# An expert layer with sixteen more tokens taken row by row, plain fp32 gate products, and a shared low-half duty

## The chip, the cores and the metric

One core of one Trainium2 chip runs one program. The metric is the time of one execution in microseconds (us). The engines are named PE (TensorE), DVE (VectorE), ACT (ScalarE), POOL (GpSimd) and SP (SyncE, which only issues DMAs here).

## The reference

Two transformer blocks on 512 tokens of width 1024. The part that the change touches is the expert layer of the first block: for each token and each of 8 heads, 16 of 16,384 one-neuron experts are chosen, and

```
act = gelu(einsum('thkd,td->thk', expert_u[experts], xb))
wgt = (g * act)
out = einsum('thk,thkd->td', wgt, expert_v[experts])
```

with `g` the softmax gates. All of it is fp32, and everything downstream depends on it. A token has 128 chosen experts (8 heads by 16).

## The kernel before

Weights come in 456 tiles of 128 x 1024 fp32 (512 KB). SP loads each into one of four slots (`wraw`), ACT rounds it to fp32r (`whi`), and DVE or POOL forms the remainder (`wlo = wraw - whi`). PE then computes each product as three fp32r matmuls: high by high, high by low, low by high (`three`, L1394 to L1396). A slot is loaded again when its low half is counted in the semaphore `w_lo` (SP waits for it in `load_w`), and ACT rewrites a slot of `whi` when PE has finished the tile that used it. PE starts a tile when `w_lo` has counted it.

The expert layer has two ways to do a token.

Densely, for the first SD tokens: 128 tiles of U (`u_blocks`) give the activation of every one of the 16,384 experts for each token, ACT applies gelu and stores the result (`act_dram`, or keeps it in SBUF for the last 20 tiles). The gates are spread over the 16,384 places by a product of two one-hot matrices per token: DVE makes `OI` (index i equals row) and `OG` (index j equals column, times the gate), and PE multiplies them for four tokens at a step (`gate_group`, L1756), which gives a 128 x 128 gate matrix per token. These steps (STEPS = SD/4) run interleaved with 60 of the U tiles, the gate tiles; 5 or 6 eighths of a U tile stand on PE between two steps. ACT and DVE move the products to `GS`, SP stores them (`gate_dram`). Then 128 tiles of V follow: DVE multiplies activations by gates (`pw_product`, L2532), ACT and DVE split the product into high and low (`WH`, `WL`), and PE accumulates over all 128 tiles into its eight banks.

By rows, for the others. The last 128 tokens (one per partition) and the FT "few" tokens before them are not in SD. For these, POOL fetches exactly the rows of U that were chosen, 128 rows of 4 KB at a time (`fetch_u`, L786), DVE makes a dot product with the token (`dot`, L2342), and in the V stage POOL fetches rows of V (`fetch_v`, L793) and DVE adds them with their weight (`row_add`, L2568). A fetch serves 128 pairs of token and expert: the last block takes 128 fetches, and FT few tokens, spread over P/FT partitions each, take FT fetches. Both rings have four buffers, so a fetch waits for the dot or the addition four before it.

So SD = 384 - FT, and with FT = 16 the dense products have 368 columns, there are 92 gate steps, and 144 dots and 144 row additions.

The order of work is written out by hand, one program for each engine. Around the gate steps it is as follows. Before them DVE runs the top-k selection (`topk`) and normalizes the gates (L2439, semaphore `tk_gate`); PE waits for that after U tile 38 (counted from 0) and then transposes gates and indices (L1742 to L1744), does tile 39 and begins with the gate tiles. A DVE step is `indices_hot` (waits for the product of two steps earlier), two `gate_sum` (adding the low half of an earlier product), `gates_hot` (waits for POOL's `OJ`), and a dot every second step. A POOL step is `offsets_j` (L800, at most four ahead), a low half when one is due (60 in the 92 steps), and a fetch every second step. After the gate steps DVE takes over the low halves from tile 103 on and the remaining dots, SP issues the last stores of the gates.

## Time and profile before

| what | value |
|---|---|
| median of three runs | 2395.32 us (2394.99 to 2395.55) |
| the profiled execution's own time | 2394.86 us |
| its span in the profile | 2393.0 us |
| PE busy | 2359.3 us (99%) |
| DVE, POOL, ACT busy | 1559.5, 1249.3, 944.9 us |
| U tiles on PE | from 508.4 to 1076.7 us |
| of these the gate tiles, with the 92 gate steps | 670.3 to 964.8 us |
| V tiles on PE | 1076.7 to 1592 us |

The profile gives for each engine the time in which it executed something. Matmul records overlap: the duration of one includes the way through the array, so what a matmul costs is read from the distance between the starts of two that follow each other.

### The profile page before, as it was taken

The numbers are of one execution on the slowest core, as the hardware profiler recorded it, in microseconds if no ns is written. First come the engines' busy times: TensorE is split into PE (matmuls) and PEld (weight loads), VectorE is DVE, ScalarE is ACT, GpSimd is POOL, SyncE is SP. The second block draws the span as 40 slices with busy tenths as digits, with TensorE's granted clock in tenths as the row PEclk, the third lists the DMA queues.
The fourth block names the chain that finished last, engine by engine and source line by source line (L and its number), as shares of the span: only waits on it lengthen the run. The fifth ranks groups of instructions, "written<-read, shape, count | busy, mean of one in ns | idle before, by whom it ended". The sixth has DMA issues, their size and how long they took to land.

```text
span 2393.0 us, 35812 instructions
## 1 busy us (share of the span) xinstructions
PE 2359.3 (99%) x12844; PEld 2121.5 (89%) x12844; DVE 1559.5 (65%) x2832; ACT 944.9 (39%) x1487; POOL 1249.3 (52%) x705
## 2 busy tenths in 40 slices
PE   7999999999999999999999999999999999999998
PEld 4878888899999999999999999998778888888886
DVE  5258435789999999679999999992365225322201
ACT  4374333344555555333333334442353223222312
POOL 3305443447899999455555555444304444444443
PEclk9999999999999999999999999999999999999999
DMA  7237422338978998999999999943202222222221
GB/s 285 80 115 264 180 93 93 132 117 280 319 240 305 321 326 306 393 379 414 413 416 411 417 406 405 376 162 114 75 23 97 97 97 88 97 96 96 96 98 71
DMA packets 179614, 526.15 MB, mean 220 GB/s; under 512 B 18240, under 2 KB 70896, under 8 KB 178224
## 3 DMA queue, kind: packets, MB, share of 16 engines
q1 hardware_dynamic: 120928, 345.24, 39.7%
q0 software_dynamic: 43024, 159.14, 17.2%
q10 hardware_dynamic: 15552, 20.36, 2.4%
q8 instruction: 63, 1.03, 0.2%
q14 instruction: 47, 0.39, 0.0%
HBM read 474.93 MB, written 49.73 MB: 219 GB/s over the span
## 4 chain that ended last, share of the span: by engine, by line
PE 94%; DVE 2%; DMA 2%; POOL 1%; ACT 1%; issue 0%; SPq 0%; ACTq 0%; DVEq 0%
PE bank L1394 22%; PE bank L1396 22%; PE bank L1395 22%; PE pair L1395 6%; PE pair L1394 6%; PE pair L1396 6%; PE pair L1756 2%; DMA wraw<-in_w 1%; PE bank L1924 1%; PE pair L1535 1%; PE bank L1561 1%; PE bank L1574 1%; POOL wlo L720 1%; PE pair L1697 1%; PE bank L1915 0%; PE bank L1907 0%
## 5 line engine op out<-in xcount | busy, mean ns | idle before, releaser
L720 POOL TENSOR_TENSOR wlo<-wraw,whi 128x1024 fp32r<-128x1024 f32 x303 | 741.4, 2450 | 743.6 <-ACT whi L867 742.3
L1394 PE MATMUL bank<-HH,whi 128*128 128x512 f32 (+1 forms) x2048 | 739.3, 361 | 4.8 <-ACT T L1139 2.1
L1396 PE MATMUL bank<-HH,wlo 128*128 128x512 f32 (+1 forms) x2048 | 735.9, 359 | 0.0
L1395 PE MATMUL bank<-HL,whi 128*128 128x512 f32 (+1 forms) x2048 | 735.8, 359 | 0.0
L867 ACT ACTIVATE whi<-wraw 128x1024 fp32r<-128x1024 f32 x456 | 481.8, 1058 | 617.0 <-PE pair L1396 308.0
L1394 PEld LDWEIGHTS bank<-HH,whi 128*128 128x128 f32 x2048 | 385.1, 188 | 47.5 <-issue 7.2
L1396 PEld LDWEIGHTS bank<-HH,wlo 128*128 128x128 f32 x2048 | 384.7, 188 | 40.2
L1395 PEld LDWEIGHTS bank<-HL,whi 128*128 128x128 f32 x2048 | 385.2, 188 | 39.3 <-issue 0.2
L793 POOL DMA_INDIRECT VROW<-in_w,which x128 | 204.6, 1599 | 191.5 <-DVE YROW L2568 178.7
L2500 DVE TENSOR_TENSOR wlo<-wraw,whi 128x1024 fp32r<-128x1024 f32 x153 | 186.3, 1218 | 20.5 <-ACT whi L867 18.7
L786 POOL DMA_INDIRECT X<-in_u_rows,which x128 | 149.9, 1171 | 60.4 <-DVE dots L2342 34.3
L1394 PE MATMUL bank<-WH,whi 128*128 128x368 f32 x512 | 169.0, 330 | 0.0
L1395 PE MATMUL pair<-WL,whi 128*128 128x368 f32 x512 | 168.8, 330 | 0.0
L1394 PE MATMUL pair<-WH,whi 128*128 128x368 f32 x512 | 168.7, 329 | 0.0
L1396 PE MATMUL bank<-WH,wlo 128*128 128x368 f32 x512 | 168.4, 329 | 0.0
L1395 PE MATMUL bank<-WL,whi 128*128 128x368 f32 x512 | 168.3, 329 | 0.0
L1396 PE MATMUL pair<-WH,wlo 128*128 128x368 f32 x512 | 168.1, 328 | 0.0
L2568 DVE SCALAR_TENSOR_TENSOR YROW<-VROW,wexp,YROW 128x1024 f32<-128x1024 f32 x128 | 165.6, 1294 | 0.4 <-DMA VROW<-in_w,which 0.2
L2616 DVE TENSOR_TENSOR T<-bank,rr 128x512 f32<-128x512 f32 x60 | 41.3, 690 | 179.9 <-PE bank L1396 179.8
L2472 DVE SCALAR_TENSOR_TENSOR OG<-T,pair 128x1024 fp32r<-128x1024 f32 x92 | 111.5, 1212 | 11.7 <-POOL T L800 11.7
L1077 ACT ACTIVATE actb<-bank 128x368 f32<-128x368 f32 x108 | 51.7, 479 | 144.7 <-PE bank L1396 137.2
L1147 ACT ACTIVATE WH<-AJ 128x368 fp32r<-128x368 f32 x128 | 64.9, 507 | 81.2 <-DVE AJ L2532 74.7
(444 smaller groups left out, 3826.2 us busy)
## 6 DMA issues: line engine op xcount, KB each, us to landing
wraw<-in_w SPq DMA_DIRECT2D x456, 512.0 KB
gate_dram<-GS SPq DMA_DIRECT2D x24, 1024.0 KB
GJ<-gate_dram SPq DMA_DIRECT2D x32, 768.0 KB
act_dram<-actb ACTq DMA_DIRECT2D x108, 184.0 KB
AJ<-act_dram SPq DMA_DIRECT2D x108, 184.0 KB
adaw<-in_ada SPq DMA_DIRECT2D x32, 512.0 KB
ada<-in_ada SPq DMA_DIRECT2D x16, 512.0 KB, 14.8
NB<-in_nab POOLq DMA_DIRECT2D x4, 1024.0 KB
```

Source lines behind the costliest of these rows:

```text
L720: nc.gpsimd.tensor_tensor(wlo[:, slot, :, :].rearrange("p k c -> p (k c)"), wraw[:, slot, :, :].rearrange("p k c -> p (k c)"), whi[:, slot ...
L786: pool.indirect_dma_start(UROW[:, m % R, :], None, A["u_rows"], bass.IndirectOffsetOnAxis(row_index(0, dot_column(m)), 0)).then_inc(u_row[ ...
L793: pool.indirect_dma_start(VROW[:, n % R, :], None, A["w"].rearrange("g p c -> (g p) c"), bass.IndirectOffsetOnAxis(row_index(1, V_ROWS[n]) ...
L867: nc.scalar.activation(whi[:, slot, :, :].rearrange("p k c -> p (k c)"), wraw[:, slot, :, :].rearrange("p k c -> p (k c)"), ACT.Copy).then ...
L1077: nc.scalar.activation(actb[:, u % 2, :], bank[u % 2][:, 0:SD], ACT.Gelu_apprx_tanh).then_inc(tile_evac, 1)
L1147: nc.scalar.activation(WH[:, slot, :], AJ[:, slot, 0:SD], ACT.Copy).then_inc(pw_hi, 1)
L1394: pe.matmul(out_, ah, bh, start=first, stop=False, **kw)
L1395: pe.matmul(out_, ah, bl, start=False, stop=False, **kw)
L1396: return pe.matmul(out_, al, bh, start=False, stop=last, **kw)
L2472: nc.vector.scalar_tensor_tensor(OG[:, q % 2, :, :, :].rearrange("p w t j -> p w (t j)"), bc(oj, 1, 2), 0.0, bc(gate_window[:, P + 8 * n:P ...
L2500: nc.vector.tensor_tensor(wlo[:, slot, :, :].rearrange("p k c -> p (k c)"), wraw[:, slot, :, :].rearrange("p k c -> p (k c)"), whi[:, slot ...
L2568: nc.vector.scalar_tensor_tensor(y, VROW[:, n % R, :], w, y, ALU.mult, ALU.add).then_inc(row_added, 1)
```

## The change

Six things change together.

- FT is 32, not 16: SD is 352, there are 88 gate steps, and 160 dots and 160 row additions. A few token now lies on 4 partitions. In the V stage a few row is added after every third row of the last block, up to tile 95, where it was every seventh, up to tile 111.
- The gates are no longer split into high and low. The gate products are plain fp32 matmuls with 128 columns, four at a step, where they were fp32r matmuls with 256 columns (both halves side by side), also four. `OG` has half its width.
- ACT alone moves the products of a step to `GS`, in one copy of 512 elements; before, a step took two copies of 256 elements on ACT and two additions of the same size on DVE.
- 92 dots stand at the gate steps (46 before), 32 in the tail of the U tiles (38 before), and 8 in the V stage (32 before).
- Of the 60 low halves at the gate steps, DVE makes the 30 of odd tiles, at the step of the tile, ahead of that step's one-hot matrices. They are not counted in `w_lo` by DVE: POOL waits for DVE's own count when it comes to the low half of the next tile, and then counts with a small `memset`.
- The last gate group stands three eighths into the U tile that follows the gate tiles, where it stood behind it. The fifth block of gates is stored from load 61 on instead of 59.

```
-FT = 16
+FT = 32
...
+U_TAIL = 4 * GATE_IT + GATE_TILES + 3
+U_POOL = 103
...
-GATE_DOT = 2
-PSUM_DOTS = TOP_DOTS + STEPS // GATE_DOT
-U_DOTS = 112
+GATE_DOTS = 92
+PSUM_DOTS = TOP_DOTS + GATE_DOTS
+TAIL_DOTS = 32
+U_DOTS = PSUM_DOTS + TAIL_DOTS
...
+        def low_step(t):
+            return (t - 4 * GATE_IT - 3) * STEPS // GATE_TILES + 1
...
 # POOL
+            def vector_low(t):
+                passed[0] += 1
+                pool.wait_ge(w_low_vector, passed[0])
+                pool.wait_ge(w_lo, G0["U"] + t)
+                nc.gpsimd.memset(low_mark, 0.0).then_inc(w_lo, 1)
...
-                if (lows - gate0 - 3) * STEPS // GATE_TILES + 1 == q:
-                    lo(G0["U"] + lows, lows % R)
+                if low_step(lows) == q:
+                    if not by_vector(lows):
+                        vector_low(lows - 1)
+                        lo(G0["U"] + lows, lows % R)
                     lows += 1
-                if q >= 2 * GATE_DOT and q % GATE_DOT == 0:
+                while fetched < R + TOP_DOTS + gate_dots(max(q - 2, 0)):
                     fetch_u(fetched)
...
 # ACT
-            def gate_high(h, stored=None):
-                high = bank[4 + h % 3].rearrange("p (t w j) -> p w j t", t=2, w=2)[:, 0]
-                nc.scalar.activation(GS[:, h // 32 % 2, :, t:t + 2], high, ACT.Copy).then_inc(g_high, 1)
+            def gate_out(q):
+                act.wait_ge(g_done, q + 1)
+                nc.scalar.activation(GS[:, q // 16 % 2, :, t:t + 4], bank[4 + q % 3].rearrange("p (t j) -> p j t", t=4), ACT.Copy)\
+                    .then_inc(g_evac, 1)
...
 # PE
-                for h in (2 * q, 2 * q + 1):
-                    if h >= 3:
-                        pe.wait_ge(g_evac, h - 2)
-                    for t in range(2):
-                        mm = pe.matmul(bank[4 + h % 3][:, t * 256:t * 256 + 256], OI[:, 4 * (q % 2) + e, :],
-                                       OG[:, q % 2, :, e, :], start=True, stop=True)
+                if q >= 3:
+                    pe.wait_ge(g_evac, q - 2)
+                for e in range(4):
+                    mm = pe.matmul(bank[4 + q % 3][:, e * P:(e + 1) * P], OI[:, 4 * (q % 2) + e, :], OG[:, q % 2, e, :],
+                                   start=True, stop=True)
...
 # DVE
+            for q in range(STEPS):
+                while low[0] < U_POOL and low_step(low[0]) <= q:
+                    if by_vector(low[0]):
+                        lo(G0["U"] + low[0], low[0] % R, w_low_vector)
+                    low[0] += 1
+                indices_hot(q)
+                gates_hot(q)
+                while dotted[0] < TOP_DOTS + gate_dots(q + 1):
+                    dot()
```

DVE at the gate steps, before: `OI` and `OG` are the one-hot matrices, `GS` the two additions (numbered as two), `X,dots` the dot and `dots` the reading of its sum.

```order
L2464 TENSOR_TENSOR OI<-iota,pair 128x512
L2482 TENSOR_TENSOR GS<-pair,GS 128x128x2 x2
L2472 SCALAR_TENSOR_TENSOR OG<-T,pair 128x1024
L2464 TENSOR_TENSOR OI<-iota,pair 128x512
L2482 TENSOR_TENSOR GS<-pair,GS 128x128x2 x2
L2472 SCALAR_TENSOR_TENSOR OG<-T,pair 128x1024
L2342 ISA X,dots<-X,bank 128x1024
L2342 ISA dots 128x1
```

The same place now, two steps, of which the second has a low half in front:

```order
L2489 TENSOR_TENSOR OI<-iota,pair 128x512
L2496 SCALAR_TENSOR_TENSOR OG<-T,pair 128x512
L2371 ISA X,dots<-X,bank 128x1024
L2371 ISA dots 128x1
L2503 TENSOR_TENSOR wlo<-wraw,whi 128x1024
L2489 TENSOR_TENSOR OI<-iota,pair 128x512
L2496 SCALAR_TENSOR_TENSOR OG<-T,pair 128x512
```

The additions are gone, `OG` is half as wide, a dot stands at every step, and a low half stands before the one-hot matrices of every third step or so.

POOL at the gate steps, before: `T<-iota,T` is `offsets_j`, `wlo` a low half, `DMA` a fetch.

```order
L800 TENSOR_TENSOR T<-iota,T 128x512
L786 DMA X<-in_u_rows,which 128x1024
L800 TENSOR_TENSOR T<-iota,T 128x512
L720 TENSOR_TENSOR wlo<-wraw,whi 128x1024
L800 TENSOR_TENSOR T<-iota,T 128x512
L720 TENSOR_TENSOR wlo<-wraw,whi 128x1024
```

And now, where `MEMSET st` is the counting of DVE's low half:

```order
L814 TENSOR_TENSOR T<-iota,T 128x512
L800 DMA X<-in_u_rows,which 128x1024
L814 TENSOR_TENSOR T<-iota,T 128x512
L839 MEMSET st 128x1
L734 TENSOR_TENSOR wlo<-wraw,whi 128x1024
L800 DMA X<-in_u_rows,which 128x1024
```

There is a fetch at nearly every step and a low half at about every third.

PE around a gate group, before:

```order
L1394 MATMUL bank<-HH,whi 128x368
L1395 MATMUL bank<-HL,whi 128x368
L1396 MATMUL bank<-HH,wlo 128x368
L1756 MATMUL pair<-OG,OI 128x256 x4
L1394 MATMUL bank<-HH,whi 128x368
```

and now:

```order
L1424 MATMUL bank<-HH,whi 128x352
L1425 MATMUL bank<-HL,whi 128x352
L1426 MATMUL bank<-HH,wlo 128x352
L1784 MATMUL pair<-OG,OI 128x128 x4
L1424 MATMUL bank<-HH,whi 128x352
```

The place and number of the products stay; their width and type, and the width of the dense matmuls, change.

## Rows read from the trace of the kernel before

**Rows 1.** The page's first section: busy us (share of the span) xinstructions.

```profile
PE 2359.3 (99%) x12844; PEld 2121.5 (89%) x12844; DVE 1559.5 (65%) x2832; ACT 944.9 (39%) x1487; POOL 1249.3 (52%) x705
```

**Rows 2.** Busy times by stage: start, gate tiles, U tail, first half of V.

```profile
core 0: us, PE busy (x) PEld busy (x) DVE busy (x) ACT busy (x) POOL busy (x), PEclk, DMA share, GB/s
16.00:32.00 16.00, 14.52 (x74) 8.11 (x71) 12.47 (x19) 6.17 (x9) 3.26 (x2) 1.00 1.02 419
670.30:964.80 294.50, 292.06 (x1835) 289.58 (x1834) 278.19 (x463) 151.35 (x304) 279.98 (x198) 1.00 0.86 300
964.80:1076.70 111.90, 109.83 (x651) 109.55 (x650) 82.56 (x118) 41.85 (x60) 56.73 (x42) 0.98 1.01 386
1076.70:1320.00 243.30, 243.30 (x1459) 243.30 (x1458) 233.45 (x306) 94.34 (x126) 136.83 (x87) 1.00 1.03 414
```

**Rows 3.** Timeline of PE: start us, us, engine, line, op; 24 matmuls apart, and two borders.

```profile
599.86 0.33 PE L1394 MATMUL bank<-HH,whi 128*128 128x368 f32 x1
...
603.86 0.33 PE L1394 MATMUL bank<-HH,whi 128*128 128x368 f32 x1
...
665.36 0.27 PE L1742 MATMUL pair<-ident,gsel 128*128 128x128 f32 x1
...
670.34 0.33 PE L1394 MATMUL bank<-HH,whi 128*128 128x368 f32 x1
```

**Rows 4.** Timeline of PE: 512-column fp32r matmuls around four plain fp32 products.

```profile
419.70 0.39 PE L1394 MATMUL bank<-HH,whi 128*128 128x512 f32 x1
...
422.20 0.39 PE L1396 MATMUL bank<-HH,wlo 128*128 128x512 f32 x1
422.43 1.05 PE L1697 MATMUL pair<-T,GS 128*128 128x128 f32 x8
...
423.55 0.40 PE L1395 MATMUL bank<-HL,whi 128*128 128x512 f32 x1
```

**Rows 5.** Timeline of PE: the last gate group of the kernel before.

```profile
964.32 0.63 PE L1756 MATMUL pair<-OG,OI 128*128 128x256 f32 x4
964.78 0.33 PE L1394 MATMUL bank<-HH,whi 128*128 128x368 f32 x1
```

**Rows 6.** Timeline of DVE: the instruction that signals `tk_gate`, and the next.

```profile
663.31 1.17 DVE L2439 TENSOR_TENSOR gsel<-gsel,hs 128x512 f32<-128x512 f32 x1
666.54 0.54 DVE L2442 COPY T<-pair 128x368 f32<-128x368 f32 x1 [2.05 <-PE pair L1744]
```

**Rows 7.** Timeline of PE in the U tail: a wait, brackets name its releaser.

```profile
1003.02 0.40 PE L1394 MATMUL bank<-HH,whi 128*128 128x368 f32 x1 [2.07 <-ACT T L1139]
```

**Rows 8.** Busy times by stage, in the columns of rows 2: behind that wait.

```profile
1003.50:1006.80 3.30, 3.30 (x13) 3.30 (x11) 3.17 (x5) 1.42 (x2) 1.61 (x1) 0.50 1.07 398
```

**Rows 9.** Groups by line in 670.3 to 964.8: xcount | busy us, mean ns | idle before.

```profile
L720 POOL TENSOR_TENSOR wlo<-wraw,whi 128x1024 fp32r<-128x1024 f32 x60 | 144.7, 2412 | 4.5 <-ACT whi L867 3.8
...
L800 POOL TENSOR_TENSOR T<-iota,T 128x512 f32<-128x512 f32 x92 | 95.5, 1047 | 0.8
...
L867 ACT ACTIVATE whi<-wraw 128x1024 fp32r<-128x1024 f32 x60 | 63.7, 1062 | 28.7 <-ACT actb L1077 28.7
...
L2464 DVE TENSOR_TENSOR OI<-iota,pair 128x512 fp32r<-128x512 f32 x91 | 62.0, 681 | 1.3 <-PE pair L1756 1.2
...
L786 POOL DMA_INDIRECT X<-in_u_rows,which x42 | 40.0, 952 | 6.5 <-issue 4.6 <-DVE dots L2342 0.5
```

**Rows 10.** Timeline of DVE in the V stage: one tile with a dot and a few row.

```profile
1213.20 0.56 DVE L2532 TENSOR_TENSOR AJ<-AJ,GJ 128x384 f32<-128x384 f32 x1 [0.68 <-PE pair L1396]
1213.68 1.22 DVE L2342 CUSTOM_DVE_ANT_0 X<-X,rr 128x1024 f32<-128x1024 f32 x1
...
1214.82 1.28 DVE L2568 SCALAR_TENSOR_TENSOR YROW<-VROW,wexp,YROW 128x1024 f32<-128x1024 f32 x1
1216.20 1.28 DVE L2568 SCALAR_TENSOR_TENSOR T<-VROW,few_wexp,T 128x1024 f32<-128x1024 f32 x1
...
1218.99 0.55 DVE L2532 TENSOR_TENSOR AJ<-AJ,GJ 128x384 f32<-128x384 f32 x1
```

More of the change, by code:

```diff
@@ L76 @@
 TOP_DOTS = sum(DOTS_TOP)
-GATE_DOT = 2
-PSUM_DOTS = TOP_DOTS + STEPS // GATE_DOT
-U_DOTS = 112
+GATE_DOTS = 92
+PSUM_DOTS = TOP_DOTS + GATE_DOTS
+TAIL_DOTS = 32
+U_DOTS = PSUM_DOTS + TAIL_DOTS
 DOTS = P + FT
-V_DOT_TILES = [10 * m // 3 + 1 for m in range(32)][:DOTS - U_DOTS]
+V_DOT_TILES = [8 * m + 1 for m in range(DOTS - U_DOTS)]
 ACTS = (60, 100, 116, P)
@@ L826, in _ @@
             for t in range(lows, U_POOL):
-                lo(G0["U"] + t, t % R)
-            for k in range(fetched, U_DOTS + R):
+                if not by_vector(t):
+                    vector_low(t - 1)
+                    lo(G0["U"] + t, t % R)
+                while fetched < R + PSUM_DOTS + (t - U_TAIL + 1) * TAIL_DOTS // (P - U_TAIL):
+                    fetch_u(fetched)
+                    fetched += 1
+            u_fetches = min(U_DOTS + R, DOTS)
+            for k in range(fetched, u_fetches):
                 fetch_u(k)
@@ L1123, in _ @@
             for n in range(STEPS + 2):
-                for h in range(2 * n - 4, 2 * n - 2):
-                    if h >= 0:
-                        gate_high(h, 64 * (h // 64) if h % 32 == 0 and h >= 64 else None)
+                if n >= 2:
+                    gate_out(n - 2)
                 for u in range(units(n) // 8, units(n + 1) // 8):
@@ L1769, in _ @@
                     gate_group(n - 1)
-            u_tile(gu0 + GATE_TILES, 0)
+            u_blocks(gu0 + GATE_TILES, 0, range(3))
             gate_group(STEPS - 1)
+            u_blocks(gu0 + GATE_TILES, 0, range(3, KB))
             for u in range(1, 4):
@@ L2443, in _ @@
             nc.vector.tensor_copy(ITS[:, 0:SD], bank[4][:, 0:SD])
-            then(nc.vector.tensor_copy(GHT[:, :], bank[6][:, 0:SD]))
-            nc.vector.tensor_tensor(GLT[:, :], bank[6][:, 0:SD], GHT[:, :].bitcast(F32), ALU.subtract).then_inc(gt_split, 1)
+            nc.vector.tensor_copy(GT[:, :], bank[6][:, 0:SD]).then_inc(gt_split, 1)
             v.wait_ge(gt_split, 1)
@@ L2502, in lo @@
                                         whi[:, slot, :, :].rearrange("p k c -> p (k c)").bitcast(F32),
-                                        ALU.subtract).then_inc(w_lo, 1)
+                                        ALU.subtract).then_inc(done, 1)
+            low = [4 * GATE_IT + 3]
+            for q in range(STEPS):
+                if q % 32 == 0:
+                    window(q // 32)
+                while low[0] < U_POOL and low_step(low[0]) <= q:
[6 more added lines that the diff above has]
+                    dot()
             def expert_weights(i):
@@ L2512, in expert_weights @@
                 v.wait_ge(w_known, i + 1)
+            for t in range(low[0], U_POOL):
+                if by_vector(t):
+                    lo(G0["U"] + t, t % R, w_low_vector)
+            v.wait_ge(g_done, STEPS)
             then(nc.vector.memset(kept0[:, :, SD:TD * P], 0.0))
-            v.wait_ge(w_lo, G0["U"] + U_POOL)
-            tail_dots = U_DOTS - PSUM_DOTS
-            for t in range(U_POOL, P):
-                lo(G0["U"] + t, t % R)
-                while dotted[0] < PSUM_DOTS + (t - U_POOL + 1) * tail_dots // (P - U_POOL):
+            for t in range(U_TAIL, P):
+                if t == U_POOL:
+                    v.wait_ge(w_lo, G0["U"] + U_POOL)
+                if t >= U_POOL:
+                    lo(G0["U"] + t, t % R)
+                while dotted[0] < PSUM_DOTS + (t - U_TAIL + 1) * TAIL_DOTS // (P - U_TAIL):
                     dot()
```

64 lines of the change are left out of this document (22 added, 42 removed).

## The prediction

> **What bounds the kernel now.** I read the page's busy times first. PE is busy 99% of the span, no other engine over 65% [rows 1], so a change pays where it takes time from PE's own work or from a wait of PE. The busy times by stage say the same of the stages that the change touches: PE is busy for 292.1 of 294.5 us at the gate tiles and for all 243.3 us of the first half of V. But others are full there too: at the gate tiles DVE 278.2 and POOL 280.0 of 294.5 us, in V DVE 233.5 of 243.3 us and the DMA engines at a share of 1.03 [rows 2]. The reader is to see that PE is the bound with neighbours right behind it.
>
> Then I took the price of PE's work from distances between starts. 24 matmuls of 368 columns take 4.00 us, 166.7 ns each [rows 3]; eleven of 512 columns take 422.20 - 419.70 = 2.50 us, 227.3 ns each [rows 4]. The difference, 60.6 ns for 144 columns, is 0.42 ns a column, one column per cycle at 2.4 GHz, on top of some 13 ns. So the weight load doesn't set the distance, and 16 columns less save 6.7 ns: 160 ns, 3.84 us for a tile of 24.
>
> **The change part by part.** Times are against the profiled execution, 2394.86 us, which lies 0.46 below the median of 2395.32.
>
> *Start to gate tiles.* 39 U tiles, 0 to 38, shrink by 0.16 us each, 6.2 us. Then PE waits for `tk_gate`, which DVE signals at 663.31 + 1.17 = 664.5; PE's transposes begin at 665.36 [rows 3, 6]. DVE's selection work before that isn't touched by the change. It was done only 0.9 us before PE, and the 2.05 us that DVE then waits are for PE's transposes. So PE now comes at 659.1 and waits 5.4 us; only 0.8 of the 6.2 us is won. The wait has a second price. After a wait of 2.07 us the granted clock is 0.50 for a stretch of 3.3 us, the lower of the two levels, 1.2 GHz [rows 7, 8]; work of 1.7 us is lost in it. I take 1.7 us here as well (bounds: 0, as after shorter waits, and twice that, if a longer wait keeps the clock low longer). Tile 39 gives 0.16. Together 1.7 - 0.8 - 0.2 = +0.7 us.
>
> *Gate tiles.* From 670.34 to 964.78 stand 61 tiles and 92 gate groups, 294.4 us [rows 3, 5]. A group costs 0.46 us (964.78 - 964.32), so 61 x 4.00 + 92 x 0.46 = 286.3, and 8.1 us are waits and ragged edges. The new group is four plain fp32 products of 128 columns. The trace has this operation elsewhere: in the score products four of them stand as eight records, two passes each. From 422.20 to 423.55 are 1.35 us, of which two matmuls of 512 columns take 0.45, so four products cost 0.90 us [rows 4]. This is the central reading: the half-width plain product is dearer than the full-width fp32r one, 0.22 against 0.12 us. 88 groups cost 79.0 us where 92 cost 42.3. With 61 x 3.84 = 234.2 this is 313.2 us of PE work.
>
> Can the others keep up with 313.2 us, 3.56 a step? DVE: 88 `OI` at 0.68 and 88 `OG`, which at 512 elements I take like `OI` (bounds 0.3 and 1.2, half as much and the old full width), 92 dots at 1.14, 30 low halves at 1.2: 119.7 + 104.9 + 36.0 = 261 us, 307 at the upper bound [rows 2, 9, 10]. POOL: 88 x 1.05 + 92 x 1.11 (0.95 and some 0.16 of issue, 6.5 us of idle over 42 being the row) + 30 x 2.41 = 267 us. The `memset` isn't in the trace; its bounds are 0 and the 1.05 us of `offsets_j`, I take 0.1, so at most 298 us [rows 9]. Both fit, and the 8.1 us of waits go, since their cause was POOL's 280 and DVE's 278 of 294.5 us [rows 2].
>
> The new wait of POOL for DVE's low halves: behind it stand a low half, `offsets_j` and the fetches. DVE's low half stands before `indices_hot`, at the step of that tile, some three steps before PE needs the tile. POOL counts it one or two steps later, which leaves about two steps, 7 us. I price it at 0.
>
> DMA: the stage moved 300 GB/s x 294.5 us = 88.4 MB [rows 2]. 46 more fetches of 0.52 MB make 112.5 MB, 359 GB/s over 313 us, where the U tail, with stores in it too, ran at 386 with a share of 1.01 [rows 2]. The average fits; bursts of stores do not quite. I take 1.5 us of waits for it (bounds 0 and 13, see the second rival). Sum of the stage: 313.2 + 1.5 - 294.4 = +20.3 us.
>
> *U tail.* The 111.9 us hold 27 tiles, 108.0 us [rows 2, 3]: 3.9 us are lost, the wait of 2.07 us and the slow clock behind it, with the DMA share at 1.01 [rows 2, 7, 8]. 27 x 0.16 = 4.3 us are won. The tail has six fetches less (3.1 MB) and one store more (1 MB) than its 43.2 MB, 41.1 MB, at 386 GB/s 106.5 us against 103.7 of PE. So the wait stays; I leave it at 3.9 (bounds 0 and 8). -4.3 us.
>
> *V stage.* 128 tiles win 20.5 us if PE keeps its pace. DVE: a tile with a dot and a few row takes 1218.99 - 1213.20 = 5.79 us; the dot is 1.14 of it, the few row 1.38, the rest 3.27 [rows 10]. Up to tile 57 the average is now 3.27 + 1.38/3 + 1.14/8 = 3.87, with the two small terms (the expert weights every fourth tile, 16 elements less in a split) about 3.89 us, against 3.84 of PE: DVE is level with PE, a hair behind. To tile 95 it is 3.75, then 3.3. DMA: 414 GB/s x 243.3 us over 61 tiles is 1.65 MB a tile [rows 2]. Up to tile 57 that stays (more few rows, fewer dots, 8 KB less of activations), so 3.84 us asks for 430 GB/s, and later 413. The trace never shows the DMA engines above 419 over a stage, at a share of 1.02 [rows 2]. At 420 a tile takes 3.93, 5 us over 58 tiles, less what the four slots hold in store. I take a loss of 3 us (bounds 0, if 430 is to be had, and 8.6, if 414 is all). -17.5 us.
>
> The Trainium skill (DMA: Bandwidth & Descriptors, "Where 436 GB/s comes from") puts the ceiling of the fabric at 435 GB/s. By that the 430 would just fit, and the sum would be 3 us lower; the 414 GB/s of this trace lie below it and don't decide [rows 2].
>
> *Sum.* 0.7 + 20.3 - 4.3 - 17.5 = -0.8 us: 2394.1, and on the scale of the median 2394.5 us. What 16 columns less give in 195 tiles outside the gate stage, plain fp32 in the gate groups and the wait for `tk_gate` take back.
>
> **The rivals.**
>
> *The waits go (faster).* The tail's DMA relief of 2.1 MB is enough to keep its wait off (-3.9), V runs at PE's pace (-3), the gate stage has no waits (-1.5): 2386.1, and 2384.4 if the clock stays up after `tk_gate` as well. For it: in V, PE doesn't wait once at a share of 1.03 [rows 2]. Against: each of the three is full by its own sum.
>
> *Store bursts stall the gate stage (slower).* A block of gates is stored as four DMAs of 1 MB with four successive weight loads. In that time, 20.7 us, now stand four tiles' weights, 6 fetches, activations and stores, 10.2 MB, at 386 GB/s 26.4 us: 5.7 behind. Before it was 8.6 MB, 22.3 against 19.3 us, 3.0 behind, and ACT's waits in the stage are for its own engine, none for weights from the DMA [rows 9]. The limit is what four slots hold; if it lies right at the old backlog, five bursts cost 2.7 us each: +13.5, less the 1.5 counted, 2406.5, and a slow stretch of the clock adds 1.7 wherever a wait is near 2 us. It decides from a backlog of some 4 us. For it: the stage's average goes from 300 to 359 GB/s. Against: DVE and POOL have slack there now and weights are asked for four tiles ahead.
>
> *The count comes late (slower).* POOL passes DVE's low halves on so late that SP loads late and PE waits, say 0.3 us at each of 30: +9, 2403.5. Speaks for it that POOL is still 85% busy; against, the two steps of lead.
>
> *The plain product is cheaper than in the score products.* At the old group's 0.46 us the stage would lose 38 us of the forecast; DVE and POOL would then bound it at some 280 us, 33 below: 2361. Against it is the row, in the same conditions [rows 4]. That a plain product is not made (the change doing less than it says) would look the same.
>
> **How the numbers follow.** A measurement of this kernel can tell about 0.2%, 4.8 us, from no change: faster is below 2390.5, slower above 2400.1. Forecast 0.43, lying mostly in the middle, with 0.03 spilling over on either side at the most; the waits go 0.25; store bursts 0.22; late count 0.06; cheap product 0.04. Faster: 0.25 + 0.04 + 0.02 = 0.31; slower: 0.22 + 0.06 - 0.01 for small stalls that stay within the bound, 0.27; same 0.42. The forecast's own range is 2390 to 2400. For 8 in 10 the range takes in the first rival's 2386 with a little below, and most of the second's: 2385 to 2407.
>
> **What would show it.** Right: PE's transposes begin at about 664.6 behind a wait of over 5 us, with the clock at 0.50 behind it; 24 U or V matmuls take 3.84 us; a gate group 0.90 us; the gate stage 313 to 316 us with DVE and POOL under 90% busy; V about 494 us. Wrong: a gate group under 0.7 us, a distance of more than 160 ns between 352-column matmuls (then something other than columns sets it), ACT waiting for weights in the gate stage, or PE not waiting for `tk_gate`.

## The result, and the profile after

The changed kernel is slower: 2422.73 us (median of 4 runs, 2421.10 to 2425.34) against 2395.15 us of the kernel before on the same chip, ratio 1.0118 [1.0106, 1.0130]. The forecast was 2394.5 us with a range up to 2407.

First the page of the profile after (busy us, share of the span, instructions), which answers [rows 1]. PE works 4 us more than before, all others less, and yet the span is 28.6 us longer:

```profile
PE 2363.4 (98%) x13180; PEld 2119.3 (88%) x13180; DVE 1512.0 (62%) x2714; ACT 928.5 (38%) x1391; POOL 1228.9 (51%) x733
```

Second the stages, in the columns of [rows 2]: gate tiles, U tail, first half of V.

```profile
669.90:1016.10 346.20, 325.55 (x2171) 320.03 (x2170) 251.36 (x390) 141.29 (x210) 257.61 (x237) 0.98 0.89 313
1016.10:1127.70 111.60, 105.07 (x650) 104.23 (x649) 75.43 (x106) 39.96 (x57) 51.27 (x37) 1.00 1.01 390
1127.70:1349.00 221.30, 220.09 (x1374) 218.75 (x1373) 214.86 (x271) 85.35 (x117) 127.56 (x77) 1.00 1.02 410
```

The gate stage takes 346.2 us, and in it PE is idle for 20.7 us, DVE for 95, POOL for 89. Nobody is full and the DMA share is 0.89, lower than in the tail. A stage that no engine bounds is bounded by a chain of waits.

PE's own work in the stage is 313.2 us by the forecast, so 33.0 us are lost, 12 more than PE is idle. The granted clock accounts for most of these: it is at 0.50 in four stretches of the stage, 17.0 us in all, in which up to 8.5 us of work are lost. Each of the four goes with a wait of PE for `OG` of 1.8 to 3.1 us. The longest of them (the columns of [rows 2]):

```profile
996.00:1003.00 7.00, 6.18 (x24) 6.18 (x25) 5.44 (x10) 2.12 (x3) 6.51 (x6) 0.51 0.92 292
```

By stage (from the starts of the first U tile, U tile 40, the first U tile behind the gate tiles, the first and the last V tile):

| stage, us | before | forecast | after | `lead` | `three_lead` |
|---|---|---|---|---|---|
| start to gate tiles | 161.9 | +0.7 | 161.5 | 158.7 | 155.5 |
| gate tiles | 294.4 | +20.3 | **346.2** | 314.3 | 313.8 |
| U tail | 111.9 | -4.3 | 111.6 | 109.3 | 108.3 |
| V | 511.7 | -17.5 | 493.1 | 491.5 | 492.8 |
| rest | 804.6 | 0 | 800.7 | 800.7 | 800.7 |
| span | 2393.0 | | 2421.6 | 2382.9 | 2380.4 |

(The last two are experiments, below.) The span missed its forecast by 29.4 us. The gate tiles alone are 31.5 us over theirs, and the other four together 2.1 us under.

Third the waits from 655 to 985 us (us in total, times, longest):

```profile
ACT GS L1145 <- PE pair L1784: 93.0, 48, 6.0
DVE X L2371 <- DMA X<-in_u_rows,which: 73.8, 30, 4.9
...
POOL st L839 <- DVE wlo L2503: 48.1, 16, 5.7
...
PE pair L1784 <- DVE OG L2496: 17.5, 14, 2.5
```

PE waits for `OG` from DVE, DVE's dots (`X`) for fetched rows, POOL's counting `memset` (`st`) for DVE's low half. That these close to a ring shows in time. POOL, 20 us of the gate stage (start us, us, engine, line, op; in brackets the idle time before and its releaser):

```profile
826.76 0.95 POOL L800 DMA_INDIRECT X<-in_u_rows,which  x1 [0.16 <-issue]
827.74 1.05 POOL L814 TENSOR_TENSOR T<-iota,T 128x512 f32<-128x512 f32 x1
831.26 0.10 POOL L839 MEMSET st<- 128x1 f32 x1 [2.48 <-DVE wlo L2503]
831.31 2.39 POOL L734 TENSOR_TENSOR wlo<-wraw,whi 128x1024 fp32r<-128x1024 f32 x1
833.84 0.95 POOL L800 DMA_INDIRECT X<-in_u_rows,which  x1
...
844.12 0.10 POOL L839 MEMSET st<- 128x1 f32 x1 [3.89 <-DVE wlo L2503]
```

and DVE in the same stretch:

```profile
829.98 1.22 DVE L2503 TENSOR_TENSOR wlo<-wraw,whi 128x1024 fp32r<-128x1024 f32 x1
...
834.65 1.22 DVE L2371 CUSTOM_DVE_ANT_0 X<-X,bank 128x1024 f32<-128x1024 f32 x1
...
839.35 1.22 DVE L2371 CUSTOM_DVE_ANT_0 X<-X,bank 128x1024 f32<-128x1024 f32 x1 [3.48 <-DMA X<-in_u_rows,which]
840.50 0.68 DVE L2489 TENSOR_TENSOR OI<-iota,pair 128x512 f32<-128x512 f32 x1
...
841.69 1.22 DVE L2371 CUSTOM_DVE_ANT_0 X<-X,bank 128x1024 f32<-128x1024 f32 x1
842.83 1.22 DVE L2503 TENSOR_TENSOR wlo<-wraw,whi 128x1024 fp32r<-128x1024 f32 x1
```

Read it as one loop. DVE's low half (to 831.1) releases POOL's `memset` at 831.26; POOL's own low half stands behind it, then the fetch at 833.84. Its row lands at 839.3 (the DMA's semaphore), 5.5 us later, and the dot that needs it is the next that DVE does. Behind that dot, in order, stand `OI`, `OG`, a dot and the next low half at 842.83, which releases POOL at 844.12. That is 12.86 us for three steps, 4.29 us a step where PE's work asks for 3.56 (the mean of the stage is 346.2 / 88 = 3.93).

The 5.5 us stand on no row of POOL: the instruction takes 0.95. The Trainium skill says why (Perfetto Trace Analysis, "Summary: the profiler window per engine type"): of a DMA issued by GpSimd the profiler shows the making of descriptors, the movement of the data is hidden. The trace agrees, 0.95 us against a landing 6.9 us after issue on average.

What the forecast priced right shows in PE's timeline: 352-column matmuls start 0.16 us apart, and the group takes 693.85 - 0.16 - 692.80 = 0.89 us (forecast 160 ns and 0.90, against [rows 3, 4]):

```profile
692.64 0.32 PE L1426 MATMUL bank<-HH,wlo 128*128 128x352 f32 x1
692.80 1.05 PE L1784 MATMUL pair<-OG,OI 128*128 128x128 f32 x8
693.61 0.41 PE L1424 MATMUL bank<-HH,whi 128*128 128x352 f32 x1
693.85 0.32 PE L1425 MATMUL bank<-HL,whi 128*128 128x352 f32 x1
```

### The profile page after: what moved, and what is told of

It is laid out like the page before. It is cut to its first block, busy times and chain, and to the rows that moved or that the text cites. A ratio compares the mean times of both kernels' runs of the same rounds, so it can differ in the third digit from the quotient of the medians.

```text
span 2421.6 us, 36339 instructions
## 1 busy us (share of the span) xinstructions
PE 2363.4 (98%) x13180; PEld 2119.3 (88%) x13180; DVE 1512.0 (62%) x2714; ACT 928.5 (38%) x1391; POOL 1228.9 (51%) x733
## 3 DMA queue, kind: packets, MB, share of 16 engines
q0 software_dynamic: 47632, 175.92, 19.1%
## 4 chain that ended last, share of the span: by engine, by line
PE 71%; DVE 13%; DMA 10%; issue 3%; POOL 2%; ACT 1%; SPq 0%; ACTq 0%; DVEq 0%; POOLq 0%
PE bank L1424 17%; PE bank L1425 17%; PE bank L1426 17%; DMA X<-in_u_rows,which 5%; PE pair L1426 4%; PE pair L1424 4%; PE pair L1425 4%; DVE X L2371 3%; DMA AJ<-act_dram 2%; DVE wlo L2503 2%; POOL wlo L734 2%; DMA wraw<-in_w 1%; DVE YROW L2588 1%; PE pair L1784 1%; DVE T L2441 1%
## 5 line engine op out<-in xcount | busy, mean ns | idle before, releaser
L734 POOL TENSOR_TENSOR wlo<-wraw,whi 128x1024 fp32r<-128x1024 f32 x273 | 667.5, 2449 | 746.3 <-ACT whi L898 745.5
L2371 DVE CUSTOM_DVE_ANT_0 X<-X,bank 128x1024 f32<-128x1024 f32 x120 | 145.8, 1215 | 90.9 <-DMA X<-in_u_rows,which 90.8
L1424 PE MATMUL bank<-WH,whi 128*128 128x352 f32 x512 | 166.1, 324 | 2.2 <-DVE wlo L2503 1.0
L1424 PE MATMUL pair<-WH,whi 128*128 128x352 f32 x512 | 165.0, 322 | 0.0
L1425 PE MATMUL bank<-WL,whi 128*128 128x352 f32 x512 | 164.7, 322 | 0.0
L1425 PE MATMUL pair<-WL,whi 128*128 128x352 f32 x512 | 164.7, 322 | 0.0
L1426 PE MATMUL pair<-WH,wlo 128*128 128x352 f32 x512 | 164.7, 322 | 0.0
L1426 PE MATMUL bank<-WH,wlo 128*128 128x352 f32 x512 | 164.7, 322 | 0.0
L1177 ACT ACTIVATE WH<-AJ 128x352 fp32r<-128x352 f32 x128 | 63.8, 498 | 217.3 <-DVE AJ L2552 208.4
L1784 PE MATMUL pair<-OG,OI 128*128 128x128 f32 x704 | 97.7, 283 | 20.6 <-DVE OG L2496 20.5
```

The lines of the kernel that those rows point to most:

```text
L734: nc.gpsimd.tensor_tensor(wlo[:, slot, :, :].rearrange("p k c -> p (k c)"), wraw[:, slot, :, :].rearrange("p k c -> p (k c)"), whi[:, slot ...
L1177: nc.scalar.activation(WH[:, slot, :], AJ[:, slot, 0:SD], ACT.Copy).then_inc(pw_hi, 1)
L1424: pe.matmul(out_, ah, bh, start=first, stop=False, **kw)
L1425: pe.matmul(out_, ah, bl, start=False, stop=False, **kw)
L1426: return pe.matmul(out_, al, bh, start=False, stop=last, **kw)
L1784: mm = pe.matmul(bank[4 + q % 3][:, e * P:(e + 1) * P], OI[:, 4 * (q % 2) + e, :], OG[:, q % 2, e, :], start=True, stop=True)
```

## Experiments

All edits are to the changed kernel unless said otherwise. The kernel before ran beside them at 2394.5 to 2395.7 us in every group. "Expected" is what was on record before the run.

### fetch_first: fetches ahead of the low halves in POOL's step

```
 # POOL, step q
+    while fetched < R + TOP_DOTS + gate_dots(max(q - 2, 0)): fetch_u(fetched)
     if low_step(lows) == q: ... vector_low / lo ...
-    while fetched < R + TOP_DOTS + gate_dots(max(q - 2, 0)): fetch_u(fetched)
```

> The changed kernel with one edit: in a POOL step the fetches of U rows stand before the wait for VectorE's low half and POOL's own low half, not behind them. Theory (a ring through two engines): POOL waits for DVE's low half, does its own (2.4 us), and only then fetches; the row lands 6.8 us later; DVE's dot waits for it, and the next low half of DVE stands behind that dot. The edit takes POOL's wait and its low half out of the ring: the gate tiles take 315 to 325 us instead of 346.1, DVE's waits for rows fall from 73.8 us to under 20, the time is 2392 to 2403 us. Rival (the DMA is too full at the store bursts, so rows are late wherever they are issued): 340 to 346 us, 2417 to 2423 us.

Measured: 2391.43 us, 0.9988 [0.9978, 0.9997], gate stage 320.3, as the theory had it, and the time 0.6 us below its range; DVE's waits for rows fall, but not under the 20 us expected. The fetch no longer stands behind a low half that waits; from 655 to 985 us the waits shrink to

```profile
DVE X L2371 <- DMA X<-in_u_rows,which: 31.2, 25, 2.7
...
POOL st L839 <- DVE wlo L2503: 10.3, 8, 2.3
```

POOL's wait for DVE, which nothing in the edit touches, went with the waits for rows. It was a part of the ring, and no cause apart from it.

### apart: DVE's low halves counted apart, POOL doesn't wait

```
+def wait_low(engine, g):      # PE and SP, for the gate tiles
...
+    if n % 2 == 0: engine.wait_ge(w_low_vector, n // 2 + 1)
+    else: engine.wait_ge(w_lo, first + (n + 1) // 2)
...
-    vector_low(lows - 1)      # POOL: no wait, no memset
...
```

> The changed kernel with DVE's low halves counted apart: POOL doesn't wait for them, PE and SP wait for DVE's own semaphore at odd tiles, and the two counts are joined behind the gate tiles. The order on every engine stays but for POOL's 30 memsets. Theory (ring through POOL's wait): without that wait POOL fetches up to one step earlier, and the gate tiles take 315 to 328 us instead of 346.1; 2392 to 2405 us. Rival (DMA too full): 340 to 346 us, 2417 to 2423 us. A second rival, that only POOL's own low half ahead of the fetch matters and not the wait for DVE's: 335 us or more.

Measured: 2418.64 us, 1.0104 [1.0087, 1.0121], gate stage 344.2. The theory expected 315 to 328 us and missed. With the suspected wait gone, 2 us of the stage are won. POOL waits for something else in the same place, ACT's rounding of the tile (`whi`); on ACT that stands behind `actb`, which waits for PE's tile, and PE waits for `OG` (22.4 us here). So the ring closes through PE instead (655 to 1010 us):

```profile
ACT actb L1109 <- PE bank L1427: 72.1, 51, 7.5
DVE X L2372 <- DMA X<-in_u_rows,which: 67.0, 34, 4.8
POOL wlo L746 <- ACT whi L899: 61.0, 30, 7.1
```

By itself 344.2 us lies in the ranges of both rivals, the full DMA (340 to 346) and POOL's own low half ahead of the fetch (335 or more). `lead`, next, tells them apart.

### lead: each fetch one step earlier, nothing else

```
-    while fetched < R + TOP_DOTS + gate_dots(max(q - 2, 0)):
+    while fetched < R + TOP_DOTS + gate_dots(max(q - 1, 0)):
```

> Edit: the changed kernel with one constant altered: at each gate step GpSimd issues the fetches that it otherwise issues one step later (q - 1 for q - 2). Fetches stay behind the low halves, and GpSimd still waits for VectorE's low halves and counts them. If the step of lead is the missing piece by itself (the dots of the kernel as changed wait because the row is asked for one step too late): gate stage 314 to 322 us, total 2390 to 2399. If the counting on GpSimd keeps its own ring alive (fetch behind the count, count behind VectorE's low half, low half behind the dot, dot behind the row): gate stage 328 us or more, total over 2404. In the kernel with the low halves counted apart the same step took the stage from 344.2 to 313.7 us.

Measured: 2385.47 us, 0.9965 [0.9951, 0.9979], gate stage 314.3, at the low end of the first expectation; the time is 4.5 us below its range. One constant turns the change from 1.2% slower to 0.35% faster. From 655 to 985 us the waits are:

```profile
DVE X L2371 <- DMA X<-in_u_rows,which: 27.8, 24, 2.8
...
POOL st L839 <- DVE wlo L2503: 7.1, 6, 1.4
```

and POOL in the stretch of before: three fetches are issued between the low halves as in the kernel after, but another one stands ahead of the `memset` that it wasn't ahead of, so the row that the next dot needs is already under way.

```profile
825.85 0.94 POOL L800 DMA_INDIRECT X<-in_u_rows,which  x1 [0.31 <-issue]
826.81 1.05 POOL L814 TENSOR_TENSOR T<-iota,T 128x512 f32<-128x512 f32 x1
829.01 0.10 POOL L839 MEMSET st<- 128x1 f32 x1 [1.15 <-DVE wlo L2503]
829.07 2.40 POOL L734 TENSOR_TENSOR wlo<-wraw,whi 128x1024 fp32r<-128x1024 f32 x1
831.61 0.95 POOL L800 DMA_INDIRECT X<-in_u_rows,which  x1
```

The transfers themselves are no faster: a row lands 7.1 us after its issue on average, 6.9 in the kernel after, and the DMA engines move more, 349 GB/s against 313. So a full DMA was not what held the kernel after. Nor does every row come in time: 29 of the 92 dots of the gate steps still wait for theirs (34 in the kernel after), but for 27 us together and not 90, and DVE, busy for 257.8 of the stage's 314.3 us, has that much slack. PE's waits for `OG`, 17.5 us in the kernel after, are down to one of 1.1.

POOL's wait for DVE's count stays in the program and costs next to nothing here: without it (apart_lead, below, one run) the stage takes 313.7 us against 314.3 and the kernel 2386.54 us against 2385.47.

### apart_lead, three, three_lead, apart_lead_swap, ff_swap_lead: the remedies combined

`swap` puts U tile 39 on PE ahead of its wait for `tk_gate`; the names say which edits are joined (`three` is apart, fetches in front and swap; `ff` is fetches in front). The stage is read from one profiled execution of each, the time is the median of all.

> Edit: low halves of VectorE counted apart, the fetches still behind the low halves of their step but each issued one step earlier. Ring theory: the row lands up to 3.5 us earlier, so VectorE's waits for rows shrink from 69 us to some 30 and the gate stage from 344 us to 325 to 335, total 2400 to 2410. Rival (what matters is that the fetch stands behind GpSimd's low half, which itself waits for ScalarE's rounding and through it for PE; a step more of lead only moves the wait): the stage stays at 340 to 345 us, total about 2418.

> Edit: the low halves of VectorE are counted apart, the fetches stand ahead of the low halves in a step, tile 39 ahead of the wait for the selection; fetches at the place the changed kernel gives them, one step later than in three_lead. It differs from three_lead by that one step alone, and from ff_swap_lead by the counting and the step. Ring theory (what costs time is how late a row lands, and counting apart takes GpSimd's wait for VectorE out of the same ring): gate stage some 316 to 318 us against 313.8 of three_lead, total 2383 to 2386. Rival (with the fetches in front the counting is what mattered, the step of lead is worth nothing): gate stage 314, total 2380 to 2382. Second rival (the step of lead is needed, the counting is not): gate stage 320, as with the fetches in front alone, total about 2387.

> The same as the kernel with the fetches in front, one step earlier, and tile 39 ahead of the wait, and in addition DVE's low halves are counted apart, so that POOL doesn't wait for them. Theory (rows are what DVE waits for, the count plays no part once fetches stand in front): within 2 us of the kernel without this edit. Rival (POOL's wait for DVE's count still costs): 3 us or more below it.

> Edit: low halves counted apart, one step of lead for the fetches, tile 39 ahead of PE's wait for the selection; fetches behind the low halves of their step, as in the changed kernel. It differs from three_lead only in the fetches' place within the step. If that place is worth nothing once there is a step of lead: gate stage 313 to 315 us, total 2379 to 2382, the same as three_lead. If it matters: gate stage over 317 us and total over 2384.

> The changed kernel with three edits: fetches ahead of the low halves in a POOL step, each fetch also one step earlier, and U tile 39 ahead of the wait for the normalized gates. Theory: what sets the pace of the gate stage is the time from the issue of a fetch to the dot that uses it (8.8 us on average in the run with the fetches in front, of which 7.4 us are the landing), so one step (3.6 us) more of lead ends DVE's waits for rows (32.6 us there): the gate tiles take 313 to 317 us instead of 320.3, tile 39 gives another 4 to 5 us, 2381 to 2386 us. Rival (POOL now waits for the dot that frees the buffer, since the ring has four, so the lead can't grow): 320 us, 2386 to 2390 us.

| kernel | apart | in front | lead | swap | gate stage | median us, ratio |
|---|---|---|---|---|---|---|
| after | | | | | 346.2 | 2422.73, 1.0118 |
| apart | x | | | | 344.2 | 2418.64, 1.0104 |
| fetch_first | | x | | | 320.3 | 2391.43, 0.9988 |
| lead | | | x | | 314.3 | 2385.47, 0.9965 |
| apart_lead | x | | x | | 313.7 | 2386.54, one run |
| apart_lead_swap | x | | x | x | 316.2 | 2386.03, 0.9966 [0.9953, 0.9978] |
| ff_swap_lead | | x | x | x | 317.9 | 2392.57, 0.9990 [0.9980, 1.0000] |
| three | x | x | | x | 327.5 | 2392.62, 0.9988 [0.9978, 0.9998] |
| three_lead | x | x | x | x | 313.8 | **2380.80, 0.9939 [0.9923, 0.9956]** |

With `lead` the stage is 313.7 to 317.9 in every row, against 313.2 of PE's own work; without it, 320 to 346. Most of the finer expectations missed. apart_lead was expected at 325 to 335 and is better. The finer order isn't additive: three, with two remedies more than fetch_first, is no faster (2392.62 against 2391.43 us; its stage of 327.5 us is from the slowest of its ten runs) and lies outside all three of its expectations. apart_lead_swap is 5 us slower than three_lead, on the side of its expectation by which the fetches' place still matters, though its stage of 316.2 lies between the two. ff_swap_lead missed its 2381 to 2386, and three_lead, which differs from it by the counting alone, is 12 us faster where under 2 were expected: with the fetches in front, POOL's wait for the count does cost, as the rival on record had it. The traces show where to look. ACT's waits for weights from the DMA, from 655 to 985 us, first in ff_swap_lead, then in three_lead:

```profile
ACT whi L898 <- DMA wraw<-in_w: 28.3, 12, 4.7
```

```profile
ACT whi L899 <- DMA wraw<-in_w: 1.5, 2, 1.0
```

That is the chain of the prediction's rival "the count comes late" (a late count, a late load); in fetch_first the same wait is 18.3 us, in the kernel after 1.5. How it becomes 12 us isn't shown: 4 of them are in the stage and 4.5 in the tail. The three kernels with fetches in front that are not three_lead also scatter most from run to run, 2387 to 2398 us, and why stays open. The best version, three_lead, beats both kernels.

### swap: tile 39 ahead of the wait for the selection

```
+    u_tile(G0["U"] + 4 * LEAD_IT + 3, 3)
     pe.wait_ge(tk_gate, 1)
     ... transposes ...
-    u_tile(G0["U"] + 4 * LEAD_IT + 3, 3)
```

> The changed kernel with U tile 39 ahead of PE's wait for the normalized gates instead of behind the transposes. PE waited 2.95 us there, and the granted clock was 0.50 for 6.8 us. Theory: the tile fills the wait, the clock stays up, and about 3 + 3.4 us less are lost up to tile 40, -5 to -6 us in all, 2417 us; the gate tiles keep their 346 us, since their pace is set elsewhere. Rival: the transposes come later for DVE, so the first gate group waits and nothing is won, 2422 to 2424 us.

Measured: 2416.80 us, 1.0090 [1.0073, 1.0107]; start to gate tiles 155.5 us, 6.0 less than after. PE doesn't wait there and its clock stays up (16 us around the place; the columns of [rows 2]):

```profile
652.00:668.00 16.00, 16.00 (x105) 15.98 (x104) 12.67 (x18) 7.53 (x10) 15.47 (x9) 1.00 0.97 357
```

So of the 6.0 us, 2.95 were PE's idleness, and the other 3.0 go with the slow clock. The gate stage keeps its 345.8 us, as expected.

### plain_alone: only the plain gate products

FT = 16 and 46 dots as before, all low halves of the gate stage on POOL; the plain fp32 groups and ACT's single copy stay.

```
-FT = 32
+FT = 16
...
-GATE_DOTS = 92
+GATE_DOTS = 46
...
-            return t % 2 == 1      # by_vector: whose low half DVE makes
+            return False
...
```

> One part of the change alone, on 16 few tokens as before: plain fp32 gate products of 128 columns, moved out by ACT alone, with all low halves on POOL, 46 dots at the gate steps, 38 in the tail, 32 in V. Theory (a plain group costs 0.90 us, the old one 0.46): 61 x 4.00 + 92 x 0.90 = 326.8 us at the gate tiles instead of 294.4, and few waits since POOL needs 280 us and DVE less than before: 2425 to 2430 us. Rival (the plain product is cheaper than its price in the score products, and the loss of the change is all waiting): 290 to 300 us at the gate tiles, 2391 to 2400 us.

Measured: 2422.91 us, 1.0122 [1.0105, 1.0139]; gate stage 326.2 us with PE busy in all of it, where 61 x 4.00 + 92 x 0.90 = 326.8 was worked out:

```profile
670.30:996.50 326.20, 326.20 (x2202) 326.20 (x2202) 173.55 (x281) 144.04 (x214) 280.94 (x198) 1.00 0.80 273
```

This is the price of the plain product free of every wait, and it stands as forecast. The time is 2 us below its range because the tail took 108.0 us, 27 x 4.00, without the 3.9 us that the kernel before loses there.

### rows_alone: only the sixteen tokens, on the kernel before

```
-FT = 16
+FT = 32
...
-U_DOTS = 112
+U_DOTS = 124
...
```

> Edit: the kernel before with sixteen more tokens by rows and nothing else: split fp32r gates of 256 columns, all low halves of the gate stage on GpSimd, 44 dots there as before, 52 in the tail, 36 in the V stage. PE's work in the gate stage is 61 x 3.84 + 88 x 0.46 = 274.7 us. By theory VectorE (its 278 us before, four steps fewer: 266 and two dots less) and GpSimd set it at some 281 to 285 us, 10 to 13 below before; the tail has 14 dots more, 7 MB and 16 us of VectorE, and comes to 118 to 130 us against 111.9; V has 28 more dots than the changed kernel at 1.14 us each with VectorE already level with PE, 505 to 520 us. Total 2385 to 2405. Rival (the ring of row fetch and dot costs here too, since the two-per-step pace of before is kept but every product is shorter): gate stage at 294 or more, total over 2405.

Measured: 2422.41 us, 1.0115 [1.0097, 1.0133]: gate 285.5 us as expected, but tail 134.9 and V 525.3, both over the expected ranges, and the time 17 us over its own. The rival's time (over 2405) came true without its cause, a gate stage of 294 or more. In the tail the DMA engines are full, DVE isn't, the columns again those of [rows 2]:

```profile
955.40:1090.30 134.90, 111.65 (x650) 107.60 (x649) 99.94 (x146) 42.19 (x60) 74.50 (x56) 0.94 1.01 389
```

Each of these two parts alone costs 27 to 28 us, and the whole change with `lead` wins 9. What I read from the stages, without a run for it: the gate stage made long by plain products, 314 us at a DMA share of 0.96, is where there is room for the fetches and dots that sixteen more tokens bring; in rows_alone more of them stand in the tail and in V.

### d46: half the dots at the gate steps, six more in the tail, the rest in V

```
-GATE_DOTS = 92
+GATE_DOTS = 46
-TAIL_DOTS = 32
+TAIL_DOTS = 38
-V_DOT_TILES = [8 * m + 1 for m in range(DOTS - U_DOTS)]
+V_DOT_TILES = [11 * m // 5 + 1 for m in range(DOTS - U_DOTS)]
```

> The changed kernel with 46 dots at the gate steps instead of 92, 38 in the tail and 48 in the V stage; nothing else is moved, the fetches stand behind the waits as in the changed kernel. Theory (the ring closes through the row that a dot waits for): with a dot at every second step four buffers are eight steps of lead, the ring opens, DVE hardly waits for rows, and the gate tiles take 313 to 318 us instead of 346.1; the V stage gets slower, since DVE then needs 3.27 + 0.46 + 0.51 = 4.24 us a tile up to tile 95 where PE needs 3.84. Rival (the pace is set by the low halves and their count, not by rows): 335 to 346 us at the gate tiles.

Measured: 2437.39 us (one run). Gate stage 312.9 us with POOL's counting as in the kernel after, so the counting is harmless where rows are fetched 19.1 us ahead (it also halves the stage's fetches, so by itself it doesn't set the ring apart from a full DMA). But V takes 545.7 us: with 40 more dots and their fetches there, DVE is busy for 231.3 of its first 240.9 us at a DMA share of 1.03, and PE for 221.4.

### ff_narrow and three_narrow: one-hot matrices in fp32r, the gates' low parts left out

```
-OI = a2("OI", [P, 8, P])
-OG = a2("OG", [P, 2, 4, P])
+OI = a2("OI", [P, 8, P], FR)
+OG = a2("OG", [P, 2, 4, P], FR)
```

> The changed kernel with the fetches in front, and the gate products in fp32r with 128 columns instead of plain fp32 (the gates are rounded to fp32r and the low part is left out). Theory (a plain fp32 product goes through the array in two passes of two cycles a column, an fp32r product of any width in one cycle a column): a group costs 4 x (128/2.4 + 13 ns) = 0.27 us instead of 0.90 us, and the gate tiles take 61 x 3.84 + 88 x 0.27 = 258 us of PE, so DVE or POOL bounds them at 280 to 300 us. Rival (a narrow fp32r product costs what a plain one does): a group of 0.9 us and 320 us.

> Edit: three_lead with the one-hot matrices in fp32r, so that the gate products are single-pass 128-column matmuls; the low parts of the gates are left out of the result. PE's own work in the gate stage is 61 x 3.84 + 88 x 0.447 = 273.6 us; VectorE's is about 261 us and GpSimd's about 267 us. If the ring of row fetch, dot and one-hot matrices is no longer what sets the pace, the gate stage comes to 276 to 285 us and the total to 2345 to 2355. If the ring was only hidden by the longer gate groups (in the narrow run with the old counting the stage stayed at 317.9 us, 44 us above PE's work), the stage stays at 300 us or more and the total at 2367 or more.

Measured: ff_narrow 2397.41 us (one run), gate stage 317.9; three_narrow 2376.03 us, 0.9920 [0.9902, 0.9938], gate stage 306.4, 21 us over its first expectation and within the second (300 or more: the ring was only hidden). The stage of ff_narrow is at its rival's 320, not for the rival's reason: its group takes 0.45 us, neither 0.27 nor 0.9. In three_narrow four products take 736.70 - 0.16 - 736.10 = 0.44 us:

```profile
736.10 0.56 PE L1785 MATMUL pair<-OG,OI 128*128 128x128 f32 x4
736.49 0.37 PE L1425 MATMUL bank<-HH,whi 128*128 128x352 f32 x1
736.70 0.32 PE L1426 MATMUL bank<-HL,whi 128*128 128x352 f32 x1
```

With half of PE's gate work gone only 7 us are won over three_lead. What stands behind PE then is close together: DVE and POOL (busy 274.2 and 275.6), the DMA at a share of 0.99 (the columns of [rows 2]), and waits again, PE 20.1 us for `OG`, DVE 18.7 us for rows, ACT 37.3 us for weights (655 to 985 us):

```profile
663.80:970.20 306.40, 286.23 (x1819) 279.70 (x1817) 274.22 (x402) 139.09 (x209) 275.63 (x212) 0.98 0.99 360
```

Which of these sets the 306.4 us no run takes apart.

## Why the prediction was wrong, point by point

**The step that failed** is in *Gate tiles*: "Can the others keep up ... Both fit", with the sentence "Behind it stand a low half, `offsets_j` and the fetches ... I price it at 0". The busy sums were right or high (DVE forecast 261, measured 251 in the stage, POOL 267 and 258). What was never worked out is the time from a fetch's issue to its dot. In the kernel before a fetch was issued 17.3 us ahead of its dot, and its row landed after 6.9 us: 10 us to spare, read off as nothing because no wait of it showed. With a fetch for every step, each issued some two steps ahead and often behind a low half, the mean lead in the kernel after is 8.2 us against the same 6.9 of landing (up to 11.0), and this lead already contains the time that late dots waited. Of the 92 dots, 34 wait for their row. No slack is left, the row is late whenever POOL is late, and since DVE works in order, POOL is late because DVE was. `lead` and `d46` show it from two sides: one step more (with the wait and the count kept) gives 314.3, half the dots give 312.9. (The mean time from issue to dot is only 8.9 us in `lead`, since the dots no longer wait so long; the waits tell the two kernels apart, the mean doesn't.) `apart`, which removes the wait and keeps the lead, gives 344.2. The rival "the count comes late" had the right instruction in view and the wrong chain: it went from the count to the loads of SP and priced 9 us; the chain goes from the count to the fetches. Behind the waits stands the clock's share, up to 8.5 of the 33 us, which the prediction had priced in its rival of store bursts but not in its sum.

**DMA in the gate stage.** The rival of the store bursts did not decide: with `lead` the same stores go out in a stage of 314.3 us at 349 GB/s. The price of 1.5 us for all waits is near what three_lead and `lead` show (0.6 and 1.1 over PE's 313.2).

**PE's prices** held: 160 ns, 0.89 us a group, 326.2 against 326.8 for plain_alone.

**Start to gate tiles**: forecast +0.7, measured -0.4, by two errors against each other. PE came at 659.48 (forecast 659.1), but DVE signalled at 662.38, not 664.5 [rows 6]:

```profile
661.63 0.75 DVE L2468 TENSOR_TENSOR gsel<-gsel,hs 128x512 f32<-128x512 f32 x1
```

so the wait was 2.95 us and not 5.4. Behind it the clock was at 0.50 for 6.8 us, which costs 3.4 us, the upper bound, not 1.7:

```profile
661.50:668.40 6.90, 5.96 (x23) 5.97 (x24) 3.46 (x9) 0.99 (x1) 6.72 (x5) 0.51 0.91 330
```

"DVE's selection work before that isn't touched" was wrong by 2.1 us; only 0.4 of it is the last instruction itself (0.75 against 1.17). It comes with the sixteen tokens and not with the gate products: the same instruction ends at 662.1 in rows_alone and at 664.3 in plain_alone. Why is not shown.

**U tail**: forecast -4.3 with the loss of 3.9 kept; measured -0.3. PE is busy for 105.1 of 111.6 us, and the DMA moved 390 GB/s x 111.6 = 43.5 MB, not 41.1. Where the gate stage ends on time the tail takes 108.3 us (three_lead), 109.3 (`lead`) or 112.8 (ff_swap_lead), at DMA shares of 1.00 to 1.02; so what of the miss came out of the gate stage stays open.

**V**: forecast -17.5, measured -18.6. 410 GB/s over the first half, no wait of weight; 5.4 us above 127 x 3.84 where 3.7 stood above 127 x 4.00.

**The rest**: -3.9 us that the forecast didn't have. PE's work in it is the same, 793.3 and 793.2 us. These are the stretches from the last V tile, of before and after:

```profile
1588.40:2393.00 804.60, 793.32 (x3605) 648.56 (x3603) 274.08 (x374) 263.83 (x424) 324.46 (x139) 1.00 0.26 88
```

```profile
1620.90:2421.60 800.70, 793.17 (x3605) 648.41 (x3603) 274.07 (x374) 263.65 (x424) 324.53 (x139) 1.00 0.27 89
```

All kernels with FT = 32 have 800.7 to 801.2, both with FT = 16 have 804.6. The difference lies behind the last output's DMA: before, the program ends 4.2 us after that has landed, and after the change 0.4 us. Why FT bears on it isn't known.

Without the ring the forecast would have been too high rather than too low: `lead`, the change with its fetches in time, is at 2385.5, 9 us under the forecast and at the place of the first rival (2386.1), but by luck. Of these 9 us, 3.9 are the unexplained rest and 3.9 lie ahead of the gate tiles, where the wait was shorter and the clock stayed up; of what that rival named V came (2.7) and, in its second figure of 2384.4, the clock, but the tail kept its loss.

## What to carry to other kernels

When a change makes a consumer of transfers more frequent, work out for one transfer the time from issue to landing and the time from issue to use, before and after; busy shares and bytes do not contain it, and a slack of 10 us shows in no wait. Ask of every new wait what stands behind it in the queue and whether that, through in-order engines, leads back to what it waits for. If nobody is full in a stage and the waits name three engines in turn, look for the ring and move its cheapest member earlier: taking away the most conspicuous wait (57 us of POOL) won 2 us of the stage, moving the fetch one step won 32. Then look at the other orders too, since remedies that help alone didn't add up here.

## What the runs showed of the hardware

- An fp32r matmul of 128 columns is hardly cheaper than one of 256: four of 128 columns take 0.44 us (ff_narrow 0.45), four of 256 columns 0.46 [rows 5].
- A pass of plain fp32 takes twice the time per column. The eight passes of a gate group take 0.89 us, 0.11 each at 128 columns. The kernel before has plain products of several widths later on; four passes (two products) take 0.43 us each at 512 columns, 0.22 at 256 and 0.11 at 128, read from the starts of what follows them:

```profile
1722.17 1.88 PE L1924 MATMUL bank<-T,RV 128*128 128x512 f32 x4
1723.89 0.55 PE L1907 MATMUL bank<-AV,T 128*128 128x64 f32 x4
...
1729.38 1.03 PE L1924 MATMUL bank<-T,RV 128*128 128x256 f32 x4
1730.25 1.00 PE L1907 MATMUL bank<-AV,T 128*128 128x64 f32 x8
...
1732.99 0.61 PE L1924 MATMUL bank<-T,RV 128*128 128x128 f32 x4
1733.44 0.78 PE L1907 MATMUL bank<-AV,T 128*128 128x64 f32 x6
```

  So the plain product is dear by its two passes and by the price of each, some 0.84 ns a column from 256 columns on, where fp32r matmuls from 352 to 512 have 0.42 and 13 ns on top.
- The Trainium skill (TensorE: Matmul & The Clock Gate, "Step-by-step: what each phase is for") has purely one cycle per column. At 352, 368 and 512 columns the fp32r distances agree with that but for 13 ns, at 128 they don't (53 ns by that rule, 110 measured), and the passes of plain fp32 don't at any of these widths.
- A row fetch of 0.5 MB lands 6.9 us after its issue on average in the gate stages before and after, 10.3 and 11.0 at most, at DMA shares of 0.86 and 0.89; in the experiments the mean is 6.3 to 7.6. By the Trainium skill (DMA: Bandwidth & Descriptors, "Anatomy of one DMA — SWDGE (gpsimd) path"), 2.0 us plus bytes at 436 GB/s, it would be an estimated 3.2 us; in a loaded stage the measurement is twice that, and it is the number to plan with.
- A wait of PE of 2.95 us was followed by 6.8 us at a granted clock of 0.50 in the kernel after, one of 2.90 us at the same place in fetch_first by 3.4 us of it, and one of 2.91 us in `lead` by none. The wait's length by itself doesn't tell the second price: here 0 to 3.4 us.
